# One block less in the experts' loop of block pairs, the last block behind the loop

## The reference, cut to what matters

```python
eidx, wts = route(h, router_w, router_b)        # two experts of one group for each token
counts = jnp.bincount(flat_e, length=N_EXPERTS)
padded = (counts + MOE_BLOCK - 1) // MOE_BLOCK * MOE_BLOCK      # MOE_BLOCK = 128
def expert_block(args):                          # xblk: 128 x 1024
    xblk, e = args
    return (jax.nn.silu(xblk @ w1[e]) * (xblk @ w3[e])) @ w2[e] # 1024 -> 512 -> 1024
out = jnp.zeros((n + 1, d), h.dtype).at[tok_buf].add(yb * w_buf[:, None])
x = x + g2 * y
```

## Time and profile before

| what | value |
|---|---|
| median of 3 runs | 3457.68 us (3452.52 to 3457.75) |
| profiled execution, its time | 3458.65 us |
| its span | 3456.9 us |
| mean granted TensorE clock | 0.961 of full speed |
| TensorE matmuls busy | 3222.9 us, 93% of the span |
| VectorE busy | 1599.0 us, 46% |
| ScalarE busy | 895.5 us, 26% |
| GpSimd busy | 789.7 us, 23% |
| L2319, down-product | 379.7 us busy, 864 records |

### The profile page before, as it was taken

How to read it: one execution, slowest core, us unless ns; L and a number is a source line. 1 busy time by engine, 2 the same in 40 slices (tenths; PEclk the granted TensorE clock), 3 DMA queues, 4 the chain that set the end, 5 groups by cost and what they waited for, 6 DMA issues and landing times. The chain is left out here.

```text
span 3456.9 us, 46809 instructions
## 1 busy us (share of the span) xinstructions
PE 3222.9 (93%) x15986; PEld 2438.2 (71%) x15987; DVE 1599.0 (46%) x2411; ACT 895.5 (26%) x1684; POOL 789.7 (23%) x512
## 2 busy tenths in 40 slices
PE   7999899999999969999999999899999996899996
PEld 5877577777777856767666887587777675666674
DVE  5552266666623666335351663264111156776312
ACT  4320255111112322222222421154111132222221
POOL 0230000110111234343343041000111123455342
PEclk9999899999999979999999999799999997999998
DMA  6130343343423337757685321242111323989664
GB/s 251 58 127 29 101 127 99 126 138 129 130 77 124 110 129 266 241 161 271 203 295 168 155 104 43 92 139 65 40 49 44 146 105 139 361 309 360 205 181 134
DMA packets 164886, 521.36 MB, mean 151 GB/s; under 512 B 31858, under 2 KB 82674, under 8 KB 141428
## 3 DMA queue, kind: packets, MB, share of 16 engines
q1 hardware_dynamic: 116656, 412.66, 32.0%
q0 software_dynamic: 18432, 62.96, 7.9%
q10 hardware_dynamic: 29668, 43.99, 4.2%
HBM read 433.00 MB, written 86.87 MB: 150 GB/s over the span
## 5 line engine op out<-in xcount | busy, mean ns | idle before, releaser
L217 PE MATMUL wide<-part,part 128*128 128x512 f32 (+2 forms) x2416 | 992.2, 411 | 54.2 <-DVE part L917 15.9
L219 PE MATMUL wide<-part,part 128*128 128x512 f32 (+2 forms) x2416 | 934.3, 387 | 0.0
L218 PE MATMUL wide<-part,part 128*128 128x512 f32 (+2 forms) x2416 | 932.5, 386 | 0.0
L217 PEld LDWEIGHTS wide<-part,part 128*128 128x128 f32 x2416 | 461.9, 191 | 176.5 <-issue 68.7
L218 PEld LDWEIGHTS wide<-part,part 128*128 128x128 f32 x2416 | 462.1, 191 | 107.6 <-issue 24.4
L219 PEld LDWEIGHTS wide<-part,part 128*128 128x128 f32 x2416 | 460.7, 191 | 93.1
L2420 DVE CAST part<-place 128x2048 fp32r<-128x2048 f32 x128 | 189.3, 1479 | 425.8 <-DMA place<-in_w 419.5
L2319 PE MATMUL bank<-place,place 128*128 x864 | 379.7, 592 | 0.0
L1681 POOL TENSOR_TENSOR place<-place,place 128x512 f32 (+3 forms) x80 | 106.3, 1329 | 1107.0 <-DVE place L1650 1107.0
L2422 DVE TENSOR_TENSOR part<-place,part 128x2048 fp32r<-128x2048 f32 x128 | 314.5, 2457 | 4.4
L2319 PEld LDWEIGHTS bank<-place,place 128*128 128x128 f32 x864 | 159.9, 190 | 180.8 <-issue 180.8
(11 more groups left out here) (253 smaller groups left out, 3837.6 us busy)
## 6 DMA issues: line engine op xcount, KB each, us to landing
place<-in_w SPq DMA_DIRECT2D x124, 1024.0 KB, 15.0
place<-in_w SPq DMA_DIRECT2D x34, 2048.0 KB, 9.8
place<-in_ada_w ACTq DMA_DIRECT2D x72, 512.0 KB, 4.3
place<-in_w_gates SPq DMA_DIRECT2D x32, 640.0 KB, 4.5
place<-in_bias SPq DMA_DIRECT2D x96, 192.0 KB, 3.3
place<-in_ada_w SPq DMA_DIRECT2D x6, 2048.0 KB, 16.9
place<-in_w_rows SPq DMA_DIRECT2D x6, 2048.0 KB, 8.4
place<-in_w_gates SPq DMA_DIRECT2D x16, 768.0 KB
```

The source lines that it names most:

```text
L217: pe.matmul(out, left[0], right[0], start=first, stop=False)
L218: pe.matmul(out, left[0], right[1], start=False, stop=False)
L219: return pe.matmul(out, left[1], right[0], start=False, stop=last)
```

## The change

On TensorE, ScalarE and GpSimd a round is now done only where its second block is in use too, and the loop has MAXB//2 rounds. With R = U//2 rounds, the loop does the down side of blocks 0 to 2R-1 and the up-products of blocks 1 to 2R. Behind it, each of the three engines has straight code once: the down side of block 2R (transposes, copy to `gt`, down-product, scaling, add), with the load of its `toadd` slots. That code has the same helpers that the body now uses. The counts that other engines wait for follow: the next stage waits for 3 + 2R adds in place of 2 + 2*((U+1)//2).

```diff
@@ SyncE, in arrive_and_project and in combine @@
-                sp.wait_ge(s["y_added"], (used + 1) // 2 * 32 + 32)
+                sp.wait_ge(s["y_added"], used // 2 * 32 + 48)
@@ experts @@
-    ROUNDS = (MAXB + 1) // 2
+    ROUNDS = MAXB // 2
...
         with eng.Fori(0, ROUNDS) as r:
-            with eng.If(used > r * 2):
+            with eng.If(used > r * 2 + 1):
                 body(r)
@@ TensorE: the body calls turn_gated and down where it had their lines @@
+            def turn_gated(r, b):
+                pe.wait_ge(s_g, r * 2 + (b + 2))
+                pe.wait_ge(s_gc, r * 2 + (b + 1))
+                for j in range(4):
+                    mm = pe.transpose(banks[4][:, j * P:(j + 1) * P], gl[:, j * P:(j + 1) * P], ident[:])
+                mm.then_inc(s_tg, 1)
+
+            def down(r, b, e, slot):
+                evens, odds = pe.snap(e // 2 * 16 + 32), pe.snap((e + 1) // 2 * 16 + 16)
+                pe.wait_ge(s_w2[0], evens)
+                pe.wait_ge(s_w2[1], odds)
+                pe.wait_ge(s_gc, r * 2 + (b + 2))
+                for h in range(2):
+                    pe.wait_ge(s_yc, r * 4 + (2 * b + h + 1))
+                    for k in range(4):
+                        mm = pe.matmul(banks[6 + h][:], gt[:, k, :],
+                                       w2[:, bass.ds(slot, 1), k, h * 512:(h + 1) * 512]
+                                       .rearrange("p o n -> p (o n)"), start=k == 0, stop=k == 3)
+                    mm.then_inc(s_y, 1)
...
             used = rounds(pe, body)
-            pe.wait_ge(s_h1, (used + 1) // 2 * 2 + 2)
-            pe.wait_ge(s_h3, (used + 1) // 2 * 2 + 2)
-            pe.wait_ge(s_y, (used + 1) // 2 * 4 + 2)
-            pe.sem_inc(s_h1, 1)
-            pe.sem_inc(s_h3, 1)
+            R = pe.snap(used // 2)
+            e = pe.value_load(plan[0:1, bass.ds(R * 2 + PLAN_EXPERT, 1)], min_val=0, max_val=EXP - 1)
+            turn_gated(R, 0)
+            down(R, 0, e, pe.snap(e % 2, min_val=0, max_val=1))
+
+            pe.wait_ge(s_h1, R * 2 + 2)
+            pe.wait_ge(s_h3, R * 2 + 2)
+            pe.wait_ge(s_y, R * 4 + 4)
+            pe.sem_inc(s_h1, 2)
+            pe.sem_inc(s_h3, 2)
             pe.sem_inc(s_y, 4)
             if not last:
-                pe.wait_ge(s_yc, (used + 1) // 2 * 4 + 2)
+                pe.wait_ge(s_yc, R * 4 + 4)
@@ ScalarE: the body calls load_to_add, copy_gated and copy_y where it had their lines @@
+            def load_to_add(r, b):
+                act.wait_ge(s_add, r * 32 + (16 * b + 16))
+                apart(act, s_done)
+                load_tokens(toadd[b], r * 2 + b, s_is[b])
+
+            def copy_gated(r, b):
+                act.wait_ge(s_tg, r * 2 + (b + 1))
+                act.activation(gt.rearrange("p a b -> p (a b)"), banks[4][:], ACT.Copy).then_inc(s_gc, 1)
+
+            def copy_y(r, b):
+                act.wait_ge(s_is[b], r * 16 + 32)
+                for h in range(2):
+                    act.wait_ge(s_y, r * 4 + (2 * b + h + 3))
+                    act.activation(yb[b][:, h * 512:(h + 1) * 512], banks[6 + h][:], ACT.Copy, scale=weight[b])\
+                        .then_inc(s_yc, 1)
...
             used = rounds(act, body)
+            R = act.snap(used // 2)
+            load_to_add(R, 0)
+            copy_gated(R, 0)
+            copy_y(R, 0)
@@ GpSimd: the body calls add_block where it had its lines @@
+            def add_block(r, b):
+                pool.wait_ge(s_yc, r * 4 + (2 * b + 4))
+                pool.wait_ge(s_add, r * 32 + (16 * b + 32))
+                apart(pool, s_pass)
+                add_rows(b)
...
-            rounds(pool, body)
+            used = rounds(pool, body)
+            add_block(pool.snap(used // 2), 0)
```

More of the change, by code:

```diff
@@ L2298, in body @@
                 for b in range(2):
-                    e = experts_of[b]
-                    evens, odds = pe.snap(e // 2 * 16 + 32), pe.snap((e + 1) // 2 * 16 + 16)
                     pe.wait_ge(s_xl, r * 4 + (2 * b + 4))
@@ L2304, in body @@
                     turn_slots(0, b, r * 2 + (b + 2))
[L2305 to L2309, removed]
+                    turn_gated(r, b)
                     pe.wait_ge(s_3c, r * 2 + (b + 2))
@@ L2312, in body @@
                     turn_slots(1, b, r * 2 + (b + 2))
[L2313 to L2322, removed]
-            used = rounds(pe, body)
-            pe.wait_ge(s_h1, (used + 1) // 2 * 2 + 2)
-            pe.wait_ge(s_h3, (used + 1) // 2 * 2 + 2)
-            pe.wait_ge(s_y, (used + 1) // 2 * 4 + 2)
-            pe.sem_inc(s_h1, 1)
-            pe.sem_inc(s_h3, 1)
+                    down(r, b, experts_of[b], slots[b])
+            used = rounds(pe, body)
+            R = pe.snap(used // 2)
[7 more added lines that the diff above has]
+            pe.sem_inc(s_h3, 2)
             pe.sem_inc(s_y, 4)
             if not last:
-                pe.wait_ge(s_yc, (used + 1) // 2 * 4 + 2)
+                pe.wait_ge(s_yc, R * 4 + 4)
                 apart(pe, s_tail)
@@ L2384, in body @@
                     load_tokens(togather[b], r * 2 + (b + 4), s_ig[b])
-                    act.wait_ge(s_add, r * 32 + (16 * b + 16))
-                    apart(act, s_done)
-                    load_tokens(toadd[b], r * 2 + b, s_is[b])
+                    load_to_add(r, b)
                     silu(r * 2 + (b + 1))
                     copy_turned(0, b, r * 2 + (b + 2))
-                    act.wait_ge(s_tg, r * 2 + (b + 1))
-                    act.activation(gt.rearrange("p a b -> p (a b)"), banks[4][:], ACT.Copy).then_inc(s_gc, 1)
+                    copy_gated(r, b)
                     copy_h3(r * 2 + (b + 1))
                     copy_turned(1, b, r * 2 + (b + 2))
[L2394 to L2398, removed]
+                    copy_y(r, b)
             used = rounds(act, body)
+            R = act.snap(used // 2)
+            load_to_add(R, 0)
+            copy_gated(R, 0)
+            copy_y(R, 0)
             if not last:
@@ L2405, in _ @@
             for b in range(2):
-                act.wait_ge(s_ig[b], ((used + 1) // 2) * 16 + 32)
-                act.wait_ge(s_xb[b], ((used + 1) // 2) * 16 + 32)
+                act.wait_ge(s_ig[b], R * 16 + 32)
+                act.wait_ge(s_xb[b], R * 16 + 32)
             apart(act, s_done)
@@ L2499, in body @@
                     gather_rows(b)
[L2500 to L2503, removed]
-            rounds(pool, body)
+                    add_block(r, b)
+            used = rounds(pool, body)
+            add_block(pool.snap(used // 2), 0)
 def combine(s, layer, last):
```

## The result

The changed kernel took 3406.41 us (median of 4 runs, 3403.97 to 3407.88) against 3456.28 us (4 runs) of the kernel before: ratio 0.9858, 95% interval 0.9843 to 0.9874, 49.9 us less. Run twice more, it was 50.6 and 49.8 us under the kernel before, run beside it. The forecast was 3402, its range 3396 to 3412.

A forecast was written before the change was run, and what follows sets the result against it. TensorE's work was taken to bound the experts' loop; each layer loses a 38.3 us round and gains a 10.5 us tail, saving 27.8, so 3458.65 - 2 x 27.8 = 3403.05 profiled, 3402 us median, range 3396 to 3412.

The forecast's parts named there:

- The bound: Experts' loop: TensorE's work sets the time up to its last block; the stage's end hangs on ScalarE's last scaling copy.
- Odd counts: Blocks in use, U, are 29 in layer 0 and 23 in layer 1, so each layer loses a round of 38.3 us.
- the wrong parity: Rival: U even, no round goes and the tail adds 10.5 per layer; 3479 for both (0.03), 3440 with one odd (0.01).
- The tail: Chain behind the loop, from block 27's last scaling copy to block 28's: 10.5 us, bounds 9.0 and 12.1.
- g: ScalarE's stretch between scaling copy and copy into `gt`, leaving the loop and issuing the `toadd` load: 2.0 us, 0.5 to 3.6.
- the rival of the low clock: Tail's down-product at 1.2 GHz after TensorE's rest, 13.1 for 7.07: +6 per layer, 3408 or 3414; chance 0.12.
- The sign that I had named for the clock: In the tail's down-product, 16 matmul records taking more than 7.1 us would show the clock assumption wrong.
- Late code: Rival: code behind the loop fetched only when reached, ScalarE and TensorE wait; +4 to +7, 3406 to 3409; chance 0.12.
- What could be late instead: Five other waits around the tail: earlier add, VectorE's preparation, SyncE's loads, `load_to_add`'s wait, SyncE's wait for adds; all expected covered.
- The add before: Block 27's add must land before the tail's add on GpSimd: 1852.9 against 1854.3, cover 1.4 us, no cost.
- `scale1`: VectorE's preparation of layer 1, needed by TensorE's first row product: ends at 1850.80, last copy 1853.4, cover 2.6 us.
- The sum: Whole kernel: profiled execution 3458.65 less 2 x 27.8 is 3403.05, so 3402 us for the median.

## Why the prediction was right, and where it was off

*The bound.* Right. TensorE's loop was the whole of the stage, and two blocks less of it are worth 38.3 us per layer: from the first down-product to block 27's last scaling copy it took 524.8 us in both traces, and in layer 1 of the kernel without a tail the load of `acc` kept its distance from the last scaling copy (11.18 for 11.25).

*Odd counts.* Right, by the records. The kernel with no round less shows what the wrong parity would have cost.

*The tail.* Mis-sized: 10.5 forecast, with bounds 9.0 and 12.1; the six tails of the changed kernel took 13.1 to 14.4, 13.8 on the mean. By its terms, in layer 0's first trace: copy 0.69 (0.69 forecast), g 2.70 (2.0, bound 3.6), copy into `gt` 0.60 (0.62), TensorE's reaction 0.40 (0.15), down-product to its last copy 10.03 (7.07). The term that was mis-sized most is the last, by 2.96, and it failed as the rival of the low clock had it: I let TensorE stand 2.5 us, and the rest was 3.98. About 0.5 of that is the transposes, which I put beside ScalarE's work and which ran ahead of it, at once; the other 0.95 is g and TensorE's reaction, both too small in the forecast. The sign that I had named for the clock, 16 records in more than 7.1 us, was there with 9.99. The rival was priced at 6 per layer, on a product cold from end to end. The clock came back within it, and the excess was 1.6 to 3.0 us. What I had given 0.12 happened in all 9 tails that rested for 4 us. So there was luck in the number. The low clock came in both layers, which the forecast had at 3414 and had left outside its range; the time fell into the range only because a part of each product ran at the full clock, where I had priced all of it at the low one.

*g.* Inside its bounds, 0.7 off. Its parts are now seen: 1.4 from the scaling copy's end until the loop is left, 1.3 for the slot load that stands ahead of the copy. Leaving begins beside the scaling copy and takes 1.9 us in all, by the queue's own instructions: three skipped rounds of about 0.6 in layer 0, four of about 0.45 in layer 1. Why a round is skipped faster in layer 1 no run shows. The second part is a matter of order alone; moved, it costs nothing, which I had not asked.

*Late code.* A packet of instructions was fetched on the same queue as in the earlier trace rows. The stretch from 1842 to 1845.5 has none; it falls into the one from 1845.5 to 1846:

```profile
q8 instruction: 1, 0.02, 25.1%
```

By then the down-product had been running since 1844.33, and ScalarE had left its loop at least 3.7 us before. ScalarE's queue has no gap for a fetch either: from the scaling copy's start to the load's issue no two of its instructions are more than 0.21 us apart. And TensorE followed the copy into `gt` by 0.40 us in both layers. So the fetch lay beside the work. Nor did it slow the product: in layer 1 no packet of instructions was fetched from 3351 to 3364, and the product ran at the low clock there too. The Trainium skill ("Runtime: NRT & Kernel Launch", Instruction fetch mechanics) says that a taken branch to a target outside the two pages held stalls until that page is fetched. This trace shows no such stall on the tail's chain, which is what the rival would have needed; whether a branch here left those pages no run shows.

*What could be late instead.* All five stayed covered. Two were called rightly as next in line. The add before landed 5.4 ahead of the tail's add, where the forecast, without its 1 us to react, had 2.4; `scale1` was ready 7.6 ahead (forecast 2.6). The tail, longer by 3.9, accounts for both within 1 us. The kernel without a tail ran into the second. The landing of the slot load, which I took at 1.7, was 1.7 in layer 0 and 5.2 in layer 1; it was hidden there, and with the copy into `gt` moved ahead of it, it held back the first scaling copy but not the last.

*The sum.* Profiled executions: 3458.65 - 3406.82 = 51.8. By the tails, (38.3 - 14.4) + (38.3 - 14.2) = 48.0; of the other 3.8, 2.3 lie ahead of layer 0's first down-product (1317.4 and 1315.1) and 2.7 between the tails of the two layers, and 1.1 was lost behind the last. The first down-product's start varies from 1309.9 to 1320.3 over the 13 traces, a spread that the 3.8 lies well within. With the mean tail the saving is 49.1, and three comparisons measured 49.8 to 50.6; the forecast of 55.6 was too large by the tails.

## What to carry to other kernels

When the last step of a pipeline is taken out of its loop, price it as a chain of one engine after another, in the order of each queue, and look for what stands ahead of the waited-for instruction without need; here one slot load cost 1.3 us twice. Then ask what the engine that bounds the loop does while it waits in that chain: TensorE, at rest for 4 us, paid again with 1.6 to 3.0 us of low clock in its next work, and idle transposes of no use to the result took that away. And look in the data for how often the padding step is real: the whole gain hung on two odd counts.

## What the runs showed of the hardware

In all 9 tails in which TensorE rested for 3.96 to 4.02 us, its next product ran at 1.2 GHz for 3.2 to 5.8 us, and took longer by half of that time. In seven the clock was low from the product's start, in the two of the kernel with no round less it fell 0.2 and 1.4 us after it. After 2.7 us of rest it fell in one tail and not in the other; after 1.05 us and less it fell in none of ten.

With nothing ahead of its first copy behind the loop, ScalarE took 1.38 or 1.39 us from its last copy's end to it past three skipped rounds (layer 0), and 1.36 to 1.43 past four (layer 1).

An indirect add issued while VectorE was splitting weights held GpSimd for 3.56 us, beside 1.58 with VectorE at rest; no run changes the one alone.
